# The last tile's final normalisation, shared between VectorE and ScalarE, with one part of it stored by token

## The reference, cut to what matters

```python
def _rmsnorm(x, g):
    x32 = x.astype(jnp.float32)
    y = x32 * lax.rsqrt(jnp.mean(x32 * x32, axis=-1, keepdims=True) + EPS)
    return (y * g.astype(jnp.float32)).astype(x.dtype)
...
    merged = jax.nn.sigmoid(m_a) * y_a + jax.nn.sigmoid(m_b) * y_b
    out = x + merged @ w_out
...
    y_prompt = _rmsnorm(yp, final_norm_g)
    y_sample = _rmsnorm(ys, final_norm_g)
```

## Time and profile before

| | before |
|---|---|
| runs | 1374.36, 1374.6, 1375.0 us |
| span of the profiled execution (first to last instruction) | 1372.1 us |
| TensorE busy | 1359.5 us, 99% of the span |
| TensorE's granted clock, mean over the span | 0.998 of full speed |
| last instruction of the last product (L521) starts | 1361.36 us |
| last store issued | 1369.21 us |

### The profile page before, as it was taken

How to read it: one execution, slowest core, us unless ns; L and a number is a source line. 1 busy time by engine, 2 the same in 40 slices (tenths; PEclk the granted TensorE clock), 3 DMA queues, 4 the chain that set the end, 5 groups by cost and what they waited for, 6 DMA issues and landing times.

```text
span 1372.1 us, 21266 instructions
## 1 busy us (share of the span) xinstructions
PE 1359.5 (99%) x8272; PEld 1345.2 (98%) x8272; DVE 932.0 (68%) x1642; ACT 685.6 (50%) x992; POOL 198.4 (14%) x200
## 2 busy tenths in 40 slices
PE   9999999999999999999999999999999999999997
PEld 7999999999999999999999999999999999999997
DVE  7899655668975456788844567987445689964443
ACT  6565444355664344556643445665433556653332
POOL 2003021110031211001212110012220200130001
PEclk9999999999999999999999999999999999999999
DMA  6544533246535333465363335653532476534338
GB/s 207 140 131 127 208 122 122 94 130 200 143 108 212 118 123 107 129 193 147 98 222 110 121 110 144 171 156 126 189 122 96 136 170 205 178 108 173 118 100 94
DMA packets 140259, 195.91 MB, mean 143 GB/s; under 512 B 83712, under 2 KB 100480, under 8 KB 138496
## 3 DMA queue, kind: packets, MB, share of 16 engines
q1 hardware_dynamic: 140160, 194.56, 47.1%
HBM read 174.91 MB, written 19.61 MB: 142 GB/s over the span
## 4 chain that ended last, share of the span: by engine, by line
PE 92%; DVE 5%; DMA 1%; issue 1%; ACT 1%; SPq 0%; DVEq 0%; ACTq 0%
PE Z L519 29%; PE Z L521 28%; PE Z L520 28%; DVE wlo L1038 1%; DMA wraw<-w_all 1%; PE B L575 1%; PE B L668 1%; PE B L658 1%; PE B L552 0%; DVE xres L1441 0%; DVE snew L1198 0%; DVE h_b L1078 0%; PE B L519 0%; PE B L521 0%; PE B L520 0%
## 5 line engine op out<-in xcount | busy, mean ns | idle before, releaser
L1038 DVE TENSOR_TENSOR wlo<-wraw,whi 128x1024 fp32r<-128x1024 f32 x280 | 367.0, 1311 | 299.7 <-ACT whi L796 299.5
L519 PE MATMUL Z<-hhi,whi 128*128 128x416 f32 x1576 | 552.7, 351 | 0.0
L520 PE MATMUL Z<-hlo,whi 128*128 128x416 f32 x1576 | 549.4, 349 | 0.0
L521 PE MATMUL Z<-hhi,wlo 128*128 128x416 f32 x1576 | 549.4, 349 | 0.0
L796 ACT ACTIVATE whi<-wraw 128x1024 fp32r<-128x1024 f32 x280 | 295.9, 1057 | 425.2 <-PE Z L521 353.0
L519 PEld LDWEIGHTS Z<-hhi,whi 128*128 128x128 f32 x1576 | 296.0, 188 | 0.9 <-issue 0.6
L520 PEld LDWEIGHTS Z<-hlo,whi 128*128 128x128 f32 x1576 | 296.0, 188 | 0.5
L521 PEld LDWEIGHTS Z<-hhi,wlo 128*128 128x128 f32 x1576 | 295.9, 188 | 0.3
L521 PE MATMUL Z<-mhi,wlo 128*128 128x416 f32 x320 | 112.3, 351 | 0.0
L520 PE MATMUL Z<-mlo,whi 128*128 128x416 f32 x320 | 111.9, 350 | 0.0
L519 PE MATMUL Z<-mhi,whi 128*128 128x416 f32 x320 | 111.5, 348 | 0.0
(11 more groups left out here) (252 smaller groups left out, 1555.2 us busy)
## 6 DMA issues: line engine op xcount, KB each, us to landing
wraw<-w_all SPq DMA_DIRECT2D x280, 512.0 KB, 3.5
xres<-xT SPq DMA_DIRECT2D x5, 1664.0 KB, 7.5
xin<-xT SPq DMA_DIRECT2D x4, 1664.0 KB, 7.8
yT<-xres SPq DMA_DIRECT2D x4, 1664.0 KB, 8.9
v_blocks<-h_vt SPq DMA_DIRECT2D x80, 52.0 KB, 3.1
vtm<-v_blocks SPq DMA_DIRECT2D x20, 192.0 KB, 3.9
ktm<-k_blocks SPq DMA_DIRECT2D x20, 192.0 KB, 3.6
k_blocks<-kt SPq DMA_DIRECT2D x64, 52.0 KB, 1.9
```

What stands on the lines that cost most here:

```text
L519: pe.matmul(out, wh, xh, start=first, stop=False)
L520: pe.matmul(out, wh, xl, start=False, stop=False)
L521: return pe.matmul(out, wl, xh, start=False, stop=final)
L1038: dve.tensor_tensor(wlo[n % RING][:], raw(t, n)[:], whi[n % RING][:].bitcast(F32), ALU.subtract).then_inc(wlo_made, 1)
```

## The change

In the tail, the eight blocks are no longer treated alike. Blocks 0 to 2 (TB = 3) are handed to ScalarE and stored by token, blocks 3 to 7 stay with VectorE.

- Weighting: during the output units of the last tile, after ScalarE has squared block j (j = 0, 1, 2), it multiplies `xres[:, j, :]` in place by the weight (new line 1007).
- Turning: TensorE transposes the three weighted blocks with the identity matrix (new function `turn`, line 682). The 416 tokens are cut into TC = 4 pieces of TR = 104, and each piece becomes 104 partitions x 384 channels in a PSUM bank of its own. That is 12 transposes. Four of them stand ahead of the two float32 matmuls on the last block's squares, and eight behind.
- Token sums: VectorE adds `yacc` and the last squares into `yall` (line 1459), and TensorE multiplies four slices of 104 tokens of it by two columns of ones (line 667). This puts each token's sum on that token's partition. ScalarE makes `yrc` of it (lines 1024, 1027), 104 x 4 numbers.
- Scaling: ScalarE copies each of the four PSUM pieces into `yt` with `yrc` as its scale per partition (line 1031).
- Stores: SP alternates between the two forms: blocks 3 and 4 to `yT`, pieces 0 and 1 of `yt` to the new output `yt_out`, blocks 5 and 6, pieces 2 and 3, block 7. The host puts `yt_out` into its place.

`yt`, `yrc`, `yall` and the split part `sql_y` lie in memory of `yhi`, which is no longer used by then.

```diff
--- before.py
+++ after.py
@@ -109,13 +109,17 @@
 TAIL = [slice(0, T // 2), slice(T // 2, T)]
+TB = 3
+TC = 4
+TR = T // TC
+TOKENS = [slice(c * TR, (c + 1) * TR) for c in range(TC)]
...
@@ -197,6 +201,10 @@
+        yt = put("yt", [TC, TB * P], F32, y_at)
+        assert 4 * TC * TB * P <= 4 * BS
+        yrc = put("yrc", [TC], F32, y_at + 4 * BS)
+        yall = put("yall", [T], F32, y_at + 5 * BS)
...
@@ -204,7 +212,7 @@
-        sql = {n: put(f"sql_{n}", [T], F32R, at) for n, at in (("head", hg[names.index("osq")]), ("y", r3 + 6 * B))}
+        sql = {n: put(f"sql_{n}", [T], F32R, at) for n, at in (("head", hg[names.index("osq")]), ("y", y_at + 6 * BS))}
...
@@ -452,13 +462,17 @@
-                    parts = [(0, 2), (2, 4), (4, 6), (6, 7), (7, KD)]
-                    for lo, hi in parts:
-                        sp.wait_ge(y_made, t * KD + hi)
+                    parts = [(3, 5, 2), (5, 7, 4), (7, KD, None)]
+                    for lo, hi, rows in parts:
+                        sp.wait_ge(y_made, t * KD + hi - TB)
                         sp.dma_start(yT[t, :, lo:hi, :], xres[:, lo:hi, :]).then_inc(y_stored, 16)
+                        if rows:
+                            sp.wait_ge(yt_made, rows)
+                            sp.dma_start(yt_out[:, rows - 2:rows, :], yt[0:TR, rows - 2:rows, :]).then_inc(yt_stored, 16)
                     sp.wait_ge(ends_stored, 48)
                     sp.wait_ge(snew_stored, 16 * H)
                     sp.wait_ge(y_stored, 16 * (TILES - 1 + len(parts)))
+                    sp.wait_ge(yt_stored, 32)
...
@@ -638,10 +652,36 @@
                     for bank, c in zip((B5, B6), TAIL):
                         pe.matmul(bank[:, c], ones_r[:], sqh[:, c], start=True, stop=False)
                         pe.matmul(bank[:, c], ones_r[:], sql["y"][:, c], start=False, stop=False)
+                    pe.wait_ge(weighted, TB)
+                    pe.wait_ge(b4_read, b4_done(t, "scores", H - 1))
+                    turn(t, 0, range(TB))
+                    turn(t, 1, range(1))
                     for i, (bank, c) in enumerate(zip((B5, B6), TAIL)):
                         pe.wait_ge(tail_squared, i + 1)
                         pe.matmul(bank[:, c], ones_r[:].bitcast(F32), ysq[(KD - 1) % 2][:, c], start=False,
                                   stop=True).then_inc(tail_summed, 1)
+                    pe.wait_ge(z_sem("out", 6), z_done(t, "out", 6))
+                    for c in range(TC):
+                        if c % 2 == 0:
+                            pe.wait_ge(yall_made, c // 2 + 1)
+                        mm = pe.matmul(z_bank("out", 6)[0:TR, 2 * c:2 * c + 2], yall[:, TOKENS[c]], ones_r[:, 0:2].bitcast(F32),
+                                       start=True, stop=True)
+                    mm.then_inc(tokens_summed, 1)
+                    turn(t, 1, range(1, TB))
+                    for c in range(2, TC):
+                        turn(t, c, range(TB))
+
+            def turn_bank(c):
+                return (B4, B7, z_bank("out", 4), z_bank("out", 5))[c]
+
+            def turn(t, c, blocks):
+
+                if c >= 2:
+                    pe.wait_ge(z_sem("out", c + 2), z_done(t, "out", c + 2))
+                for j in blocks:
+                    mm = pe.transpose(turn_bank(c)[0:TR, j * P:(j + 1) * P], xres[:, j, TOKENS[c]], ident[:])
+                if j == TB - 1:
+                    mm.then_inc(turned, 1)
...
@@ -962,6 +1002,10 @@
                         h_hi(t + 2, H_SLOT[s])
                     if kind == "out":
                         y_square(t, j)
+                    if kind == "out" and last and j < TB:
+                        act.wait_ge(ysq_made, nth(t, KD, j))
+                        act.activation(xres[:, j, :], xres[:, j, :], ACT.Copy,
+                                       scale=cst[:, C_FG + j:C_FG + j + 1]).then_inc(weighted, 1)
                 if last:
                     act.preload_act_table_set(LN_EXP)
                     for i, c in enumerate(TAIL):
@@ -976,6 +1020,16 @@
                         act.wait_ge(tail_read, i + 1)
                         ins = act.activation(yrs[:, c], yrs[:, c], ACT.Exp, scale=-0.5)
                     ins.then_inc(yrs_made, 1)
+                    act.wait_ge(tokens_summed, 1)
+                    act.activation(yrc[0:TR], z_bank("out", 6)[0:TR, 0:2 * TC:2], ACT.Ln, bias=eps_t[0:TR],
+                                   scale=1.0 / D).then_inc(yrc_made, 1)
+                    act.wait_ge(yrc_made, 1)
+                    act.activation(yrc[0:TR], yrc[0:TR], ACT.Exp, scale=-0.5).then_inc(yrc_made, 1)
+                    act.wait_ge(yrc_made, 2)
+                    for c, bank in enumerate((B4, B7, z_bank("out", 4), z_bank("out", 5))):
+                        act.wait_ge(turned, c + 1)
+                        act.activation(yt[0:TR, c, :], bank[0:TR, 0:TB * P], ACT.Copy,
+                                       scale=yrc[0:TR, c:c + 1]).then_inc(yt_made, 1)
...
@@ -1400,7 +1454,10 @@
                     for c in TAIL:
                         dve.tensor_tensor(xres[:, KD - 1, c], z_bank("out", KD - 1)[:, c], xres[:, KD - 1, c],
                                           ALU.add).then_inc(tail_made, 1)
-                    output(t, range(KD))
+                    for i, c in enumerate(TAIL):
+                        dve.wait_ge(tail_squared, i + 1)
+                        dve.tensor_tensor(yall[:, c], yacc[:, c], ysq[(KD - 1) % 2][:, c], ALU.add).then_inc(yall_made, 1)
+                    output(t, range(TB, KD))
...
@@ -1686,7 +1743,7 @@
-    outs = {"yT": x.shape, "sp_out": (P, H, P), "pp_out": (P, G, BUF), "ss_out": (H, P, NB, P),
+    outs = {"yT": x.shape, "yt_out": (TR, TC, TB * P), "sp_out": (P, H, P), "pp_out": (P, G, BUF), "ss_out": (H, P, NB, P),
             "ps_out": (P, G, NB, BUF)}
...
-    y = np.asarray(r["yT"]).transpose(0, 3, 2, 1).reshape(SEQ + SAMPLE, D)
+    y = np.asarray(r["yT"]).transpose(0, 3, 2, 1).reshape(SEQ + SAMPLE, D).copy()
+    y[-T:, 0:TB * P] = np.asarray(r["yt_out"]).transpose(1, 0, 2).reshape(T, TB * P)
```

More of the change, by code:

```diff
@@ L115, with step_kernel @@
 OUTPUT_SLOT = (5, 6, 7, 9)
-def step_kernel(nc, xT, w_all, consts, w_pool, s_in, buf_in, yT, sp_out, pp_out, ss_out, ps_out):
+def step_kernel(nc, xT, w_all, consts, w_pool, s_in, buf_in, yT, yt_out, sp_out, pp_out, ss_out, ps_out):
     with ExitStack() as ctx:
@@ L316, in step_kernel @@
         tail_made, tail_squared, tail_summed = sem("tail_made"), sem("tail_squared"), sem("tail_summed")
+        weighted, turned, yall_made, tokens_summed = sem("weighted"), sem("turned"), sem("yall_made"), sem("tokens_summed")
+        yrc_made, yt_made, yt_stored = sem("yrc_made"), sem("yt_made"), sem("yt_stored")
         z_read = [sem(f"z_read{i}") for i in range(NZ)]
```

## The result

The changed kernel took 1376.25 us (median of 21 runs, 1375.27 to 1377.15), the kernel before 1374.31 us (21 runs, 1373.34 to 1375.0). The ratio is 1.0014, with a 95% interval of 1.0008 to 1.0020: it is slower, by 1.9 us, under the 2.7 us called tellable ahead of the runs but outside its interval and above my range, which ended at 1375.9. The span of the profiled execution rose from 1372.1 to 1373.9 us. The changed kernel's profiled execution took 1376.08 us, 2.2 above its own span; the 2.5 us that the prediction carried over came from different executions and were 0.3 too many.

What follows compares the result with a forecast made beforehand. The prediction took the tail to be bound by a five-engine chain up to the first store, then a nearly gapless 1.70 MB store stream. Terms 0.05, 0 and 0.05 gave a 1372.2 us span and 1374.7 us of time; range 1373.7 to 1375.9.

Steps and rivals of the forecast that it cites:

- the 2.5 us that the prediction carried over: Gap between the profiled span of 1372.1 us and the median of 1374.6, taken as unchanged by the change.
- the start of the stream: First of the last stores in SP's queue: 0.05 us later, for the four transposes ahead of the squares' sum.
- its length: Last five stores: same 1664 KB at 370 GB/s, through after the same 4.6 us, so cost 0.
- the end: After the last store: 0.05 us; one more semaphore that SP waits on was put under 0.1 us.
- wrong altogether: Sign in the profile after: the whole span moves by over 1.5 us in either direction.
- idle engines: Store stream: 104 rows use 13 of 16 DMA engines; 0.4 us later, 1375.1 us; chance 0.2.
- Weighting: Three ScalarE passes in the last tile's output units: 1.9 us, but the last low part still 8.8 us early; cost 0.
- Transposes ahead of the last squares: Four TensorE transposes before the last squares' matmuls: 0.11 us per record, mostly in free time; cost 0.05 us.
- Token sums: Four float32 matmuls, eight records on TensorE after the last squares: 1.0 us overlapped, ending near 1364.6.
- scaled copies: ScalarE's four copies of PSUM pieces into `yt`: 0.57 us each, the last done at 1367.3.
- SP's queue: Issues of the five last stores: each holds SP 0.33 us, the last at 1367.65, 1.55 us earlier than before.
- the second rival: 104-row stores on 13 engines: busiest carries 113 KB instead of 104, stream 5.0 us, time 1375.1 us; chance 0.2.

Runs made afterwards that it cites:

- e2: Changed kernel with its two `yt` stores replaced by 128-row stores of blocks 0-1 and block 2 to `yT`, same total bytes; 1374.21 us, tail time 7.5 us.
- e7: Kernel before with its first store of blocks 0 and 1 cut in two, so block 0 goes out early; 1373.96 us, tail time 7.5 us.
- e5: Changed kernel with token pieces of 128, 128, 128 and 32 rows, six stores; 1374.12 us against 1374.14 for the kernel before, ratio 0.9999.
- e6: e5 with the store of blocks 3 and 4 cut in two, so block 3 goes out early; 1374.0 us against 1374.2, ratio 0.9997.

## Why the prediction was wrong, by its own steps

The sum had three terms: 0.05 for the start of the stream, 0 for its length, 0.05 for the end. The second failed. The step was "At 370 GB/s it is through after the same 4.6 us": it took 6.6 us. By the prediction's own signs this is "wrong altogether" (the span moved by 1.8 us, over 1.5), and a stretch of 4.9 us or more at a share below 0.9 was its sign for idle engines.

- The bound on the changed kernel was named rightly. Its tail is a chain up to the first store and then a stream bound by its engines; e2, with everything of the change but its store shape, keeps the stream at 4.5 us and the tail at 7.5. For the kernel before, the prediction read the equal landings of 2.4 to 2.5 us as stores that wait for each other. e7 speaks against it: with less queued ahead its last store took 2.5 us all the same, so that is what one store takes.
- Weighting, priced at 0: right. Its three passes moved the last low part (L1092) from 1345.18 to 1346.88, and no wait of TensorE came of it: VectorE's residuals still wait for TensorE, as the rows below show.
- Transposes ahead of the last squares, priced at 0.05: 0.61 us from the start of the first to the end of the fourth, (0.61 - 0.27) / 3 = 0.11 from one to the next as forecast. The 0.44 us of the chain's row above are only their part of the chain. They cost nothing: the float32 matmuls start 0.84 us after the last residual, as before (1362.31 - 1361.47; 1362.59 - 1361.75).
- Token sums were priced at 1.0 us and took 0.81. The scaled copies were priced at 0.57 each and follow each other every 0.5 us (two in 1.05 below). ScalarE was done at 1366.7, 0.3 us ahead of the forecast once the shift is taken off.
- SP's queue: the first three issues came as forecast. The fourth was priced at 0.33 us and held SP for 1.85, which I had no term for; e2 and e5 show that a hold alone does no harm.
- The length of the stream: the 104-row store was an operation that the trace of before did not show. I bounded it by bytes per engine alone, 113 / 104 x 4.6 = 5.0 us, in the second rival, and gave that 0.2. The rival named the right operation and one part of the cause, the engines left idle; it had the size wrong, 0.4 us for 2.0. It let each engine keep its rate, which fell from 24 to 21 GB/s per busy engine (0.7 us), and it let all of them work to the end, where the last two microseconds ran at a share of 0.47 (most of the other 1.3 us). That slow engines are what makes the others finish early is argued, not shown.

Rows of the changed kernel behind the points on weighting and on TensorE and ScalarE (timeline):

```profile
1346.88 1.22 DVE L1092 TENSOR_TENSOR wlo<-wraw,whi 128x1024 fp32r<-128x1024 f32 x1 [2.25 <-ACT whi L836]
...
1356.97 0.59 DVE L1306 TENSOR_TENSOR xres<-Z,xres 128x416 f32<-128x416 f32 x1 [3.92 <-PE Z L535]
1361.47 0.66 DVE L1455 TENSOR_TENSOR xres<-Z,xres 128x208 f32<-128x208 f32 x2 [1.13 <-PE Z L535]
```

```profile
1361.70 0.61 PE L682 MATMUL B<-ident,xres 128*104 128x128 f32 x4
1363.12 0.81 PE L667 MATMUL Z<-ones_r,yall 128*104 128x2 f32 x8
```

```profile
1364.71 1.05 ACT L1031 ACTIVATE yt<-B,yrc 104x384 f32<-104x384 f32 x2
1365.65 1.05 ACT L1031 ACTIVATE yt<-Z,yrc 104x384 f32<-104x384 f32 x2
```

The other part of the cause, the paths, I did not look for, and no upper bound of mine was wide enough for it. A store shape that a trace does not show needs a bound above from a rate, not from a count of bytes.

## What to carry to other kernels

When the last thing a kernel does is a stream of stores at a busy share near 1, faster arithmetic beside it gains nothing (e2). An earlier start gained nothing with one engine feeding the stream (e7) and 0.3 us of tail time with two (e6), too little for the times to tell. A change of layout changes the shape of the stores, and their rate is a term of the sum of its own: keep them at all 128 partitions, or measure the new shape alone first.

## What the runs showed of the hardware

- Time of a stream of five stores by the partitions that it takes: 0 to 127 4.5 us, 0 to 63 4.3, 32 to 95 3.0, 0 to 95 4.8, 0 to 111 5.4, 0 to 103 5.6, 0 to 119 5.7, 0 to 99 7.6. Dropping 8 of 128 partitions made the stream longer by a quarter.
- What a busy DMA engine moves in these streams: 24 GB/s with partitions 0 to 127 and with 32 to 95, 13 with 0 to 63, 19 to 21 with 96, 100, 104, 112 and 120 rows.
- Number of small packets per store, read as the number of engines: 16 for 128, 112, 96 and 64 rows, 15 for 120, 13 for 104, 10 for 100.
- SP is held at the issue when stores pile up: the fourth of five took 1.0 us in e2 (128 rows) and 1.85 in the changed kernel, against 0.33 in the kernel before, whose stores come 0.56 us or more apart.
- One store of 208 or 416 KB lands 2.4 to 2.5 us after its issue in the kernel before.
- Open: why seven rows per engine (112) are slower than six (96) or eight (128).
